# A two-block transformer kernel on one core: three modulation rows of layer 1 go by way of DRAM, one output piece moves behind the attention, and the pooled copies move ahead of the exponents

## The reference

```
c_act = jax.nn.silu(c)
for l in range(DEPTH):
    mod = c_act @ ada_w[l] + ada_b[l]
    shift_m, scale_m, gate_m, shift_f, scale_f, gate_f = [m[:, None, :] for m in jnp.split(mod, N_MOD, axis=-1)]
    h = rms_norm(x, g_pre_mix[l]) * (1.0 + scale_m) + shift_m
    q, k, v, u = jnp.split(h @ w_in[l] + b_in[l], ...)
    attn_out = sliding_window_attention_with_sinks(q, k, v, sinks[l])       # 8 heads of 64, window 128
    pool_out = causal_pool_mixer(u, pool_w[l], pool_scale[l])               # 4 groups of 128
    mix = jnp.concatenate([attn_out, pool_out], axis=-1) @ w_out[l]
    x = x + gate_m * rms_norm(mix, g_post_mix[l])
    h = rms_norm(x, g_pre_ffn[l]) * (1.0 + scale_f) + shift_f
    f = (jax.nn.silu(h @ w_gate[l]) * (h @ w_up[l])) @ w_down[l]
    x = x + gate_f * rms_norm(f, g_post_ffn[l])
```

## Time and profile before

| | |
|---|---|
| median of the runs | 1190.87 us |
| the profiled execution | 1189.61 us |
| its span in the trace | 1187.8 us |
| PE busy | 1145.8 us (96%) |
| DVE, ACT busy | 808.4 us (68%), 633.7 us (53%) |
| the chain that ended last | PE 86%, DVE 7%, ACT 3%, DMA 2% |
| data moved | 252.97 MB, 213 GB/s on average |

### The profile page before, as it was taken

The page is one execution under the profiler, slowest core; times in us unless marked ns, Lnnn a source line. Parts: engine busy times, 40 slices in busy tenths (PEclk is TensorE's granted clock), DMA queues, the critical chain, the costliest instruction groups (busy, mean ns, idle before and its releaser), DMA issues.

```text
span 1187.8 us, 19636 instructions
## 1 busy us (share of the span) xinstructions
PE 1145.8 (96%) x7899; PEld 1023.7 (86%) x7899; DVE 808.4 (68%) x1255; ACT 633.7 (53%) x1114; POOL 26.1 (2%) x61
## 2 busy tenths in 40 slices
PE   5999999999999999999999999999999999999997
PEld 3566999998878999999888799999989888999996
DVE  5798967796977756545676667656657757765663
ACT  3067533355567544345665656545555576555543
POOL 2200000000000000000000000000000000000000
PEclk9999999999999999999999999999999999999999
DMA  9994999997543766585343455555534434555530
GB/s 378 410 421 193 333 321 307 319 379 271 201 150 111 307 232 223 213 256 170 115 178 107 162 186 203 189 181 184 191 129 148 143 106 180 211 180 190 198 106 36
DMA packets 37305, 252.97 MB, mean 213 GB/s; under 512 B 4416, under 2 KB 4704, under 8 KB 8928
## 3 DMA queue, kind: packets, MB, share of 16 engines
q1 hardware_dynamic: 34992, 244.47, 57.5%
q0 software_dynamic: 2080, 7.25, 1.7%
q10 hardware_dynamic: 144, 0.00, 0.0%
HBM read 250.64 MB, written 1.06 MB: 212 GB/s over the span
## 4 chain that ended last, share of the span: by engine, by line
PE 86%; DVE 7%; ACT 3%; DMA 2%; issue 1%; SPq 0%; DVEq 0%; ACTq 0%
PE bank L490 25%; PE bank L492 25%; PE bank L491 25%; PE bank L497 3%; PE bank L585 2%; DMA raw_w<-weights 2%; PE bank L539 2%; DVE raw_w L1584 2%; DVE lo_w L1574 1%; ACT gtok L1136 1%; PE bank L626 1%; PE bank L926 1%; ACT prob L1249 0%; PE bank L877 0%; ACT hi_w L1131 0%
## 5 line engine op out<-in xcount | busy, mean ns | idle before, releaser
L1574 DVE TENSOR_TENSOR lo_w<-raw_w,hi_w 128x1024 fp32r<-128x1024 f32 (+3 forms) x346 | 409.2, 1209 | 123.9 <-ACT hi_w L1131 123.4
L1131 ACT ACTIVATE hi_w<-raw_w 128x1024 fp32r<-128x1024 f32 (+3 forms) x346 | 350.4, 1040 | 140.6 <-DMA raw_w<-weights 76.2
L490 PE MATMUL bank<-in_hi,lo_w 128*128 128x256 f32 x1408 | 395.6, 281 | 0.0
L492 PE MATMUL bank<-in_hi,hi_w 128*128 128x256 f32 x1408 | 392.8, 279 | 0.0
L491 PE MATMUL bank<-in_lo,hi_w 128*128 128x256 f32 x1408 | 392.7, 279 | 0.0
L490 PEld LDWEIGHTS bank<-in_hi,lo_w 128*128 128x128 f32 x1408 | 264.2, 188 | 2.6 <-issue 0.8
L491 PEld LDWEIGHTS bank<-in_lo,hi_w 128*128 128x128 f32 x1408 | 263.7, 187 | 1.9 <-issue 0.5
L492 PEld LDWEIGHTS bank<-in_hi,hi_w 128*128 128x128 f32 x1408 | 264.7, 188 | 0.0
L490 PE MATMUL bank<-hi_w,in_lo 128*128 128x256 f32 (+2 forms) x464 | 142.7, 307 | 8.1 <-DVE in_lo L1719 2.1
L492 PE MATMUL bank<-hi_w,in_hi 128*128 128x256 f32 (+2 forms) x464 | 140.0, 302 | 0.0
L491 PE MATMUL bank<-lo_w,in_hi 128*128 128x256 f32 (+2 forms) x464 | 140.0, 302 | 0.0
(11 more groups left out here) (216 smaller groups left out, 1084.5 us busy)
## 6 DMA issues: line engine op xcount, KB each, us to landing
raw_w<-weights SPq DMA_DIRECT2D x215, 1024.0 KB, 5.1
ink<-ink_w SPq DMA_DIRECT2D x8, 640.0 KB, 13.2
rows<-norm_rows POOLq DMA_DIRECT2D x5, 512.0 KB, 4.9
ink<-whole_w SPq DMA_DIRECT2D x2, 1024.0 KB, 23.3
early_out<-whole_w SPq DMA_DIRECT2D x2, 1024.0 KB, 13.5
rows<-mod_rows POOLq DMA_DIRECT2D x4, 512.0 KB, 9.3
raw_w<-weights SPq DMA_DIRECT2D x2, 832.0 KB, 4.4
const<-const_table SPq DMA_DIRECT2D x1, 1538.0 KB, 8.0
```

The source lines that it names most:

```text
L490: nc.tensor.matmul(o, st[1], mv[0], start=start, stop=False, **kw)
L492: return nc.tensor.matmul(o, st[0], mv[0], start=False, stop=stop, **kw)
L1131: nc.scalar.activation(hi_w[:, m % NSPLIT, cut], raw_view(unit)[:, cut], ACT.Identity).then_inc(*sig("hi_w", unit, i))
L1574: nc.vector.tensor_tensor(lo_w[:, m % NSPLIT, cut], raw_view(unit)[:, cut], hi_w[:, m % NSPLIT, cut].bitcast(F32), ALU.subtract).then_inc( ...
```

## The change

Five things are done. The three `spread_row` calls of layer 1 on PE and the three `row_in` on ACT go; instead POOL issues `row_out` and `row_back` for each of the rows. `row_out` of the gate and the scale stand directly behind the last `mod_row` of layer 0, so they are issued when their columns are ready, in the feed-forward of layer 0; each `row_back` waits until the slot of `rows` has been read for the last time. The piece `into_y(1, 0, ("wo", 1, 3), 1)` moves from before the attention to behind it, and `turn_prob(5)` to before `into_y(1, 0, ("wo", 1, 2), 1)`. On ACT `pooled_in` moves ahead of `exps(4)`, and `pool_hi` ahead of `exps(5)`. On DVE `shares(5)` moves ahead of `lo(("wo", 1, 3), (1,))`, and `lo(("wo", 1, 1))` ahead of `attn_lo`. The waits of DVE for a row now name the DMA that brings it.

```diff
@@ on PE, layer 1 @@
                     into_y(1, 0, ("wo", 1, 2), 0, first=True)
                     into_y(1, 0, ("wo", 1, 3), 0)
                     turn_prob(4)
+                    turn_prob(5)
                     into_y(1, 0, ("wo", 1, 2), 1, first=True)
-                    turn_prob(5)
-                    into_y(1, 0, ("wo", 1, 3), 1)
...
                 for jp in range(2):
                     attention(jp)
                 if L == 1:
-                    spread_row(L, "gate", 0)
-                    spread_row(L, "scale", 1)
-                    spread_row(L, "shift", 1)
+                    into_y(1, 0, ("wo", 1, 3), 1)
@@ on POOL @@
             mod_row(0, "gate", 1)
             mod_row(1, "shift", 0)
             mod_row(1, "scale", 0)
+            row_out(1, "gate", 0)
+            row_out(1, "scale", 1)
+            pool.wait_ge(*due("gained", "y", 0, 1, 1, 1))
+            row_back(1, "gate", 0)
             sinks_in(1)
+            pool.wait_ge(*due("scaled", ("mix", 1), 1, 1))
+            row_back(1, "scale", 1)
+            row_out(1, "shift", 1)
+            pool.wait_ge(*due("normed", ("mix", 1), 1, 1))
+            row_back(1, "shift", 1)
             pool.wait_ge(*due("normed", ("ffn", 1), 1, 1))
@@ on ACT, layer 1 @@
                     probT_in(2)
+                    pooled_in()
                     exps(4)
-                    pooled_in()
+                    pool_hi(0)
+                    pool_hi(1)
                     exps(5)
                     probT_in(3)
-                    pool_hi(0)
-                    pool_hi(1)
                     prepare(("wo", 1, 3), (1,))
...
-                    row_in(1, "gate", 0)
-                    row_in(L, "scale", 1)
-                    row_in(L, "shift", 1)
                     prepare(("gu", 1, 0))
@@ on DVE, norm() for the feed-forward; gain() and scale() likewise @@
-                            ve.wait_ge(*due("row", N[1], "shift", 1, c))
+                        ve.wait_ge(*(due("row", 0, "shift", 1, c) if N == ("ffn", 0) else due("row2", N[1], "shift", 0 if N[0] == "mix" else 1)))
@@ on DVE, layer 1 @@
                     pool_lo(0)
                     pool_lo(1)
+                    shares(5)
                     lo(("wo", 1, 3), (1,))
-                    shares(5)
                     behind(("wo", 1, 3))
                     lo(("wo", 1, 0))
+                    lo(("wo", 1, 1))
                     attn_lo()
-                    lo(("wo", 1, 1))
```

More of the change, by code:

```diff
@@ L1616, in gain @@
                     return
[L1617 to L1620, removed]
+                ve.wait_ge(*(due("row", 0, "gate", 0, c) if (L, w) == (0, 0) else due("row0", L, "gate", w)))
                 job = ("y", L, w, T, c)
@@ L1644, in scale @@
                     if T == 0:
-                        ve.wait_ge(*(due("row1", N[1], "scale", 0) if N[0] == "mix" else due("row", N[1], "scale", 1, c)))
+                        ve.wait_ge(*(due("row", 0, "scale", 1, c) if N == ("ffn", 0) else due("row1", N[1], "scale", 0 if N[0] == "mix" else 1)))
                     else:
@@ L1662, in norm @@
                         ve.wait_ge(*due("scaled", N, T, c))
-                        if N[0] == "ffn":
-                            ve.wait_ge(*due("row", N[1], "shift", 1, c))
-                        else:
-                            ve.wait_ge(*due("row2", N[1], "shift", 0))
+                        ve.wait_ge(*(due("row", 0, "shift", 1, c) if N == ("ffn", 0) else due("row2", N[1], "shift", 0 if N[0] == "mix" else 1)))
                         ins = nc.vector.scalar_tensor_tensor(dst, scaled[:, cols(c)], r, rows[:, 2, cols(c)], ALU.mult, ALU.add)
```

## The result

The changed kernel took 1194.43 us (median of 20 runs, 1188.66 to 1198.38), the kernel before 1191.14 (20 runs, 1189.76 to 1194.86): ratio 1.0025, 95% interval 1.0017 to 1.0033, so 2 to 4 us slower. It also scatters twice as far. So by the medians it is somewhere from 1 us faster to 4 us slower, and which it is differs from one set of runs to the next. 1191.2 was forecast, and 1187.0 to 1195.0 as the range.

The account below looks back on a forecast made before the run. PE, busy for 96% of the span, was taken to bound the kernel. The terms -5.4 - 0.3 + 2.8 + 3.2 sum to +0.3 us, on the median 1190.87 giving 1191.2, range 1187.0 to 1195.0 for 8 in 10.

Parts of the forecast that it names:

- The spreads and DVE: Layer 1's mixer: PE gains 5.4 us without the spreads, and DVE adds to x 0.3 us sooner.
- rival D: Layer 1's mixer: PE needs the spreads as cover, 1.3 us of the 5.4 come back, 1192.5; chance 0.05.
- The pooled copies: Layer 1's mixer: PE's 1.82 us wait moves by one piece, to the low half of ("wo", 1, 3); 0 us.
- The shift row: Layer 1's mixer norm: the row lands at 373.0, wanted at 370.2; PE waits 2.8 us more, bounds 0 and 3.7.
- rival A: Layer 1's mixer: the shift row's read finds a quiet queue, lands in 3.7 us, in time; 1188.4; chance 0.12.
- The gate and scale writes: Layer 0's feed-forward: each write holds a weight load, making layer 0's boundary 3.2 us late; bounds 0 and 10.4.
- both caught units: Weight loads the writes delay: ("gu", 0, 19), its copy moving to 257.4, and ("in", 1, 1), landing at 290.6.
- the lag is carried on: Layer 0's feed-forward: the queue does not catch up in 30 us, so the scale's column comes 5.9 us late.
- PE does not feel this yet: Layer 0's feed-forward: the late ("gu", 0, 19) copy causes no PE wait, with 2.4 us of margin.
- rival C: Layer 0: one new write holds the queue 3.6 us more, 1194.8, or both, 1198.4; chance 0.14.
- Rival B: Layer 0: the second write catches nothing, ("in", 1, 1) is through; 1188.0; chance 0.15, with the quiet-queue case 0.06.
- The clock: Whole kernel: PE's granted clock is 2.4 GHz in all 40 slices, so no term comes from it.

Follow-up runs that it names:

- e4: The changed kernel with all three rows read from an input table and none written: 5.9 us faster than the kernel before.
- e5: The kernel before with only the moved output piece and the swaps on ACT and DVE, spreads kept: 1.3 us slower by the medians.
- e2: The changed kernel with gate and scale rows read from an input table, shift row still through DRAM: 2.8 us faster than the kernel before.
- e10: e2 measured once more, on another chip: 4.1 us faster than the kernel before.
- e6: The changed kernel with columns transposed on PE and written as 8 contiguous lines, all in layer 1's mixer: 5.0 to 5.3 us faster than the kernel before.
- e8: The changed kernel measured a second time, on another chip: ratio 1.0036 to the kernel before, 4.4 us slower.
- e1: The kernel before plus only the two early gate and scale writes in layer 0, never read back: 3.5 us slower by the medians.
- e3: The changed kernel with the shift row read from an input table, both early writes kept: 2.8 us faster than the kernel before.
- e12: The changed kernel measured a third time, on another chip: ratio 0.9988 to the kernel before.
- e7: The changed kernel with gate and scale written by element in layer 1's mixer (from 306.7), shift row spread by PE: 10.8 us slower than before.

## Why the prediction came out as it did

- The spreads and DVE, -5.7: measured -5.64 in e4. Right, and so was the cover: rival D is out.
- The pooled copies, 0: right, by the pair of waits in the changed kernel and in e5.
- The shift row, +2.8: measured +2.45 (e2) and +2.51 (e10), with the clock held apart. In the three profiles of the changed kernel the wait was 3.0, 3.8 and 2.1 us longer (steps of 69.72, 70.44 and 68.74 us, against 66.69). Right, rival A is out. The prediction's upper bound of 3.7 is a slip: its longest write and longest read give 3.5. That the read took 10 us goes with the write of elements ahead of it: with loads about and none ahead, it took 3.8 in e6. Whether it is the loads which that write had held up or something else that it left, no run separates. The Trainium skill, DMA: Bandwidth & Descriptors, Queues, rings and completion order, has the engines go round robin between queues; the 3.8 us are nearer to this than I had put it, and the 10 are not explained by it.
- The gate and scale writes, +3.2: both caught units were right, the holds of 13.6 and 13.0 us too, and so was "the lag is carried on": from the gate's column to the scale's it is 6.3 us more than before, where 5.9 was forecast (5.3 to 7.4 in the six profiles). Two steps failed. The first is the start: the sum takes the gate's column at 243.91, from one profile, as fixed, and it stood at 242.6 to 247.5. Spread over the six, the cost is 1.2 to 5.9 us; that their average is the forecast's 3.2 is in part luck. The second is "PE does not feel this yet". In the profiled execution the caught unit reached ACT at 261.10 and not at 257.4, which is more than the margin of 2.4 us, and PE waited 0.75 and 0.56 us for `lo_w`; e8 has one such wait, of 0.44, and the other four none. This answers rival C in part. Its figure, 294 for ("in", 1, 1), is what the profiled execution shows, and so are waits of PE in the feed-forward, but no new write held the queue 3.6 us longer. Its threshold, an ACT wait of 5.5 us, does not follow from its sum: ACT waited 1.3 to 3.0 us for that unit, having come late itself, and the turn was up to 6.5 us late. Rival B, nothing caught, is out.
- The clock, which I put at nothing: 1.2 us behind each of the two long waits of the profiled execution (0.3 in e1, where PE waited 1.64 us). "The clock granted is the upper of its two levels, 2.4 GHz, in all 40 slices, so no term below comes from it" was read from a line too coarse for it, which hid even that kernel's own stretch at 65, and from stages without waits of this length. A wait added to PE has to be priced with what the clock does after it.

On the profiled executions these are -5.6, +3.0, +6.5 and 2 x 1.2, together 6.3 at the second turn of layer 1, and 0.8 that came later, in stages that the change does not touch, and that I did not trace to a cause. On the medians the three sets stand 3.3 and 4.4 us above before and 0.6 below. With the clock in it, the forecast's sum of +0.3 would have been about +2.5: that the measured times lie in its range is owed to the range's width, since it had no term for the clock and none for the spread between sets. Why the weights are later in one execution or on one chip than on another stays open; the extra stretch of low clock near the start in e3 and e12 is one part of it.

## What to carry to other kernels

A DMA is not priced by its bytes: 4 KB written element by element kept a saturated weight queue from 1 MB loads for 12 us, and what it costs is the missing margin of whichever load it meets, so ask at each such place which load that is and when it is due. Turn a column on PE and write whole lines, and in layer 1's mixer the same round trip through DRAM is short, does no harm, and brings nearly all that the ceiling allows (5.0 to 5.3 of 5.9 us here). And where a load has little margin, one profile of before gives one draw of its lateness: look at several, and take scatter in the time as a sign.

## What the hardware showed that I had not expected

- While a write of 1,024 elements was under way, the DMA engines were busy for 61% and moved 24 GB/s (e7, 306 to 318).
- Behind waits of 1.6 to 4.7 us PE's granted clock fell to its lower level for 3 us or more. The next turn came 0.8 to 1.2 us later behind waits of 2.5 to 4.7, and 0.3 behind those of 1.64 (e1) and 2.39 (e12). Four matmuls of no use in the wait prevented it.
- A read of one row by 128 partitions took 3.8 us among weight loads when its write was short, 3.7 with little under way, and mostly 9 to 10 (10.7 in e8) directly behind a write of elements.
